# Turning three quarters of a layer's input by VectorE squares and a DRAM exchange instead of one half

## The reference

```
def _layer(x, mem, positions, w_in, ..., w_mem_kv, w_out, ln_g, ln_b):
    (r_q, r_k, r_v, a_cq, a_ckv, a_kpe, l_x, l_v, l_o, l_i, l_f, c_q, z) = _split_cols(x @ w_in, IN_SPLITS)
    ...
    y = jnp.concatenate([ret, mla, mls, memo], axis=-1) * jax.nn.silu(z.astype(f32))
    y = y.astype(x.dtype) @ w_out
    return _layernorm(DEEPNORM_ALPHA * x + y, ln_g, ln_b)
```

## Time and profile before

| | |
|---|---|
| median of 3 runs | 889.2 us (888.85 to 889.35) |
| the profiled execution | 888.95 us, span 887.1 us |
| granted TensorE clock | 1.00 (2.4 GHz) |
| busy: TensorE, VectorE, ScalarE | 881.4, 662.7, 488.6 us |
| HBM traffic | 225 GB/s over the span |

### The profile page before, as it was taken

How to read it: one execution, slowest core, us unless ns; L and a number is a source line. 1 busy time by engine, 2 the same in 40 slices (tenths; PEclk the granted TensorE clock), 3 DMA queues, 4 the chain that set the end, 5 groups by cost and what they waited for, 6 DMA issues and landing times.

```text
span 887.1 us, 13174 instructions
## 1 busy us (share of the span) xinstructions
PE 881.4 (99%) x4516; PEld 757.0 (85%) x4516; DVE 662.7 (75%) x1326; ACT 488.6 (55%) x914; POOL 17.8 (2%) x18
## 2 busy tenths in 40 slices
PE   9999999999999999999999999999999999999997
PEld 8888998888888888888888889888888888888896
DVE  6869697878594677766679787978777878786765
ACT  6655785545455346544477566745355453565641
POOL 0000000000000000000000000000000001000001
PEclk9999999999999999999999999999999999999999
DMA  9796487547669688666677876885485874967822
GB/s 357 289 332 203 136 273 263 170 139 225 214 220 321 214 242 262 201 195 196 191 239 231 295 254 179 263 261 168 140 276 144 280 237 155 291 219 250 329 86 95
DMA packets 72402, 200.33 MB, mean 226 GB/s; under 512 B 9608, under 2 KB 24208, under 8 KB 71696
## 3 DMA queue, kind: packets, MB, share of 16 engines
q1 hardware_dynamic: 71760, 198.44, 68.8%
q10 hardware_dynamic: 576, 1.05, 0.4%
HBM read 183.43 MB, written 16.00 MB: 225 GB/s over the span
## 4 chain that ended last, share of the span: by engine, by line
PE 98%; issue 1%; ACT 0%; POOL 0%; DVE 0%; POOLq 0%; ACTq 0%; DVEq 0%
PE acc L1347 24%; PE acc L1348 24%; PE acc L1351 24%; PE acc L1362 10%; PE acc L1368 5%; PE work L1136 1%; PE work L1135 1%; PE work L1134 1%; PE work L1253 1%; PE work L1252 1%; PE work L1118 0%; PE work L1275 0%; PE work L1264 0%; PE work L1192 0%; PE work L1186 0%
## 5 line engine op out<-in xcount | busy, mean ns | idle before, releaser
L1434 DVE TENSOR_TENSOR lo<-raw,hi 128x512 fp32r<-128x512 f32 (+2 forms) x607 | 387.5, 656 | 181.6 <-ACT hi L1093 174.2
L1093 ACT ACTIVATE hi<-raw 128x512 fp32r<-128x512 f32 (+2 forms) x607 | 356.0, 604 | 297.3 <-PE acc L1351 234.7
L1347 PE MATMUL acc<-hi,xx 128*128 128x512 f32 (+2 forms) x768 | 285.5, 374 | 0.0
L1348 PE MATMUL acc<-hi,xx 128*128 128x512 f32 (+2 forms) x768 | 283.6, 372 | 0.0
L1351 PE MATMUL acc<-lo,xx 128*128 128x512 f32 (+2 forms) x768 | 223.0, 372 | 0.0
L1348 PEld LDWEIGHTS acc<-hi,xx 128*128 128x128 f32 x768 | 144.6, 188 | 23.6
L1347 PEld LDWEIGHTS acc<-hi,xx 128*128 128x128 f32 x768 | 144.6, 188 | 23.6
L1351 PEld LDWEIGHTS acc<-lo,xx 128*128 128x128 f32 x768 | 140.4, 188 | 24.6
L1362 PE MATMUL acc<-xx,hi 128*128 128x512 f32 x384 | 96.0, 392 | 0.0
L1362 PEld LDWEIGHTS acc<-xx,hi 128*128 128x128 f32 x384 | 69.3, 189 | 12.5
L1368 PEld LDWEIGHTS acc<-xx,lo 128*128 128x128 f32 x384 | 52.4, 190 | 3.7
(11 more groups left out here) (348 smaller groups left out, 965.5 us busy)
## 6 DMA issues: line engine op xcount, KB each, us to landing
raw<-in_w SPq DMA_DIRECT2D x263, 512.0 KB, 4.3
B<-turn SPq DMA_DIRECT2D x80, 128.0 KB, 4.2
raw<-in_w SPq DMA_DIRECT2D x26, 256.0 KB, 2.7
turn<-B SPq DMA_DIRECT2D x12, 512.0 KB, 5.6
raw<-in_w SPq DMA_DIRECT2D x16, 328.0 KB, 3.2
turn<-Y SPq DMA_DIRECT2D x8, 512.0 KB, 5.4
Y<-in_wuq SPq DMA_DIRECT2D x2, 1152.0 KB, 9.5
Y<-in_x_t SPq DMA_DIRECT2D x4, 512.0 KB, 8.7
```

The source lines that it names most:

```text
L1093: act.activation(place(l, t, hi), raw[:, s, (t % 2) * w:(t % 2 + 1) * w], ACT.Copy)\
L1347: pe.matmul(o, ah[:, q], hi[:, s, 0:w], start=k == 0, stop=False, skip_group_check=name == "memv")
L1348: pe.matmul(o, al[:, q], hi[:, s, 0:w], start=False, stop=False, skip_group_check=name == "memv")
L1434: dve.tensor_tensor(place(l, t, lo), raw[:, s, (t % 2) * w:(t % 2 + 1) * w], place(l, t, hi).bitcast(F32), ALU.subtract).then_inc(lo_done. ...
```

## The change

The boundary between the two ways moves from column 1024 to column 512. TensorE turns column block 0 alone (`xT` 0 and 1, both at slot 18). VectorE's squares and the DRAM exchange take blocks 1, 2 and 3: `square_x` at slots 10, 12 and 14, writes with pairs 10, 11 and 12, reads with pairs 13, 14 and 15. Each write gets a semaphore of its own, so that the reads of a block wait for its own write. `normalise` goes in the order cb 1, 2, 3, 0. `B` 6 holds the third squares and `B` 7 the turned block 1. `x_hi` and `x_lo` of j = 2 and 3 read it in SBUF and no longer a PSUM bank. The DRAM tensor `x_turn` grows from two blocks to three.

```diff
--- before.py
+++ after.py
@@ -132,7 +132,7 @@
     table.setdefault(slot, []).append(step)
 
 
-for _j in range(4):
+for _j in range(2):
     _put(LATER_PE, 18 + _j // 2 * 4, "xT", _j)
 for _h in range(HEADS):
     _put(PE_AT, (71, 75, 81, 87)[_h], "mem_scores", _h)
@@ -153,7 +153,7 @@
 
 ACT_AT = {}
 for _j in range(8):
-    _put(LATER_ACT, 8 + _j, "normalise", (4, 5, 6, 7, 0, 1, 2, 3)[_j])
+    _put(LATER_ACT, 8 + _j, "normalise", (2, 3, 4, 5, 6, 7, 0, 1)[_j])
     _put(LATER_ACT, (23, 24, 27, 28, 29, 30, 32, 33)[_j], "x_hi", _j)
     _put(FIRST_ACT, 15 + 2 * _j, "x_hi", _j)
     if _j:
@@ -185,8 +185,8 @@
 
 
 DVE_AT = {}
-_put(LATER_DVE, 11, "square_x", 2)
-_put(LATER_DVE, 13, "square_x", 3)
+for _cb in range(1, 4):
+    _put(LATER_DVE, 8 + 2 * _cb, "square_x", _cb)
 for _j in range(8):
     _put(LATER_DVE, (24, 26, 28, 30, 32, 33, 35, 37)[_j], "x_lo", _j)
     _put(FIRST_DVE, 16 + 2 * _j, "x_lo", _j)
@@ -456,11 +456,11 @@
 
         early = [Br[i][:, :].rearrange("p (a k t) -> p a k t", a=2, k=2) for i in (1, 2, 3, 0)]
 
-        x_squares, x_turned = ([B[i][:, 0:1024] for i in pair] for pair in ((4, 5), (2, 0)))
+        x_squares, x_turned = ([B[i][:, 0:1024] for i in pair] for pair in ((4, 5, 6), (7, 2, 0)))
 
         def x_block(j, n):
 
-            return x_turned[j // 2 - 2].rearrange("p (a i j r) -> p j i a r", a=4, i=NT, j=4)[:, j % 2 * 2 + n]
+            return x_turned[j // 2 - 1].rearrange("p (a i j r) -> p j i a r", a=4, i=NT, j=4)[:, j % 2 * 2 + n]
 
         def y_part(part, j):
 
@@ -543,7 +543,7 @@
         first_rows = signal("first_rows", 0)
         finished, gained, diag_done = signal("finished", 0), signal("gained", 0), signal("diag_done", 0)
         scaled, copied = signal("scaled", 0), signal("copied", 0)
-        x_squared, x_turn_out = signal("x_squared", 0), signal("x_turn_out", 0, step=16)
+        x_squared, x_turn_out = signal("x_squared", 0), [signal(f"x_turn_out{cb}", 0, step=16) for cb in (1, 2, 3)]
         stored = signal("stored", 0, step=16)
         dve_own, act_own = signal("dve_own", 0), signal("act_own", 0)
 
@@ -748,14 +748,14 @@
                         wait_job(sp, l, ("ml_q", 1))
                         sp.dma_start(B[3][:, 0:1024], a["mrow"].rearrange("h t -> (h t)").partition_broadcast(P))\
                           .then_inc(mrow_in.sem, 16)
-                    if l and m in (10, 11):
+                    if l and m in (10, 11, 12):
                         sp.wait_ge(x_squared.sem, m - 9)
-                        sp.dma_start(a["x_turn"][m - 10], x_squares[m - 10]).then_inc(x_turn_out.sem, 16)
-                    if l and m in (14, 15):
-                        sp.wait_ge(x_turn_out.sem, 2 * 16)
+                        sp.dma_start(a["x_turn"][m - 10], x_squares[m - 10]).then_inc(x_turn_out[m - 10].sem, 16)
+                    if l and m in (13, 14, 15):
+                        sp.wait_ge(x_turn_out[m - 13].sem, 16)
                         for b in range(4):
-                            sp.dma_start(x_turned[m - 14][b * 32:(b + 1) * 32, :].rearrange("c (a n) -> c a n", a=4),
-                                         a["x_turn"][m - 14, :, b * 256:(b + 1) * 256].rearrange("(a c) n -> c a n", a=4))\
+                            sp.dma_start(x_turned[m - 13][b * 32:(b + 1) * 32, :].rearrange("c (a n) -> c a n", a=4),
+                                         a["x_turn"][m - 13, :, b * 256:(b + 1) * 256].rearrange("(a c) n -> c a n", a=4))\
                               .then_inc(xT_in[m - 12].sem, 16)
                     if m in TURN_OUT_AT:
                         name = TURN_OUT_AT[m]
@@ -862,7 +862,7 @@
                 def normalise(b):
                     cb, i = divmod(b, 2)
                     blk = X[:, i, cb * 512:(cb + 1) * 512]
-                    if b == 4:
+                    if b == 2:
                         act.wait_ge(ln_done.sem, ln_done.at(l, -1))
                     act.activation(blk, blk, ACT.Identity, scale=ln_rstd[:, i:i + 1], bias=ln_shift[:, i:i + 1])\
                        .then_inc(normed.sem, 1)
@@ -879,14 +879,14 @@
                         act.activation(xh[:, 2 * j:2 * j + 2, :], xT0[:, j, :].rearrange("p (k t) -> p k t", k=2),
                                        ACT.Copy).then_inc(x_hi.sem, 1)
                         return
-                    if j < 4:
+                    if j < 2:
                         wait_job(act, l, ("xT", j))
                     else:
                         act.wait_ge(xT_in[j // 2].sem, 16 + 4 * 16)
                     act.wait_ge(cols_in.sem, cols_in.at(l, 0))
                     for k in (2 * j, 2 * j + 1):
-                        o, f = xh[:, k, :], (bank(l, ("xT", j))[:, (k % 2) * 256:(k % 2 + 1) * 256] if j < 4 else x_block(j, k % 2))
-                        m = act.activation(o if j < 4 else o.rearrange("p (i a r) -> p i a r", i=NT, a=4), f, ACT.Identity,
+                        o, f = xh[:, k, :], (bank(l, ("xT", j))[:, (k % 2) * 256:(k % 2 + 1) * 256] if j < 2 else x_block(j, k % 2))
+                        m = act.activation(o if j < 2 else o.rearrange("p (i a r) -> p i a r", i=NT, a=4), f, ACT.Identity,
                                            scale=cols[:, C_LNG + k:C_LNG + k + 1], bias=cols[:, C_LNB + k:C_LNB + k + 1])
                     m.then_inc(x_hi.sem, 1)
 
@@ -1140,7 +1140,7 @@
 
                 def xT(j):
                     pe.wait_ge(ident_in.sem, 16)
-                    pe.wait_ge(normed.sem, 2 * (j // 2) + 6)
+                    pe.wait_ge(normed.sem, 2 * (j // 2) + 8)
                     o = take("xT", j)
                     for kk in range(2):
                         for i in range(NT):
@@ -1484,11 +1484,11 @@
                         dve.wait_ge(cols_in.sem, cols_in.at(l, 0))
                         for k in (2 * j, 2 * j + 1):
                             o, f = tmp[:, (k % 2) * 256:(k % 2 + 1) * 256], \
-                                (bank(l, ("xT", j))[:, (k % 2) * 256:(k % 2 + 1) * 256] if j < 4 else x_block(j, k % 2))
-                            m = dve.tensor_scalar(o if j < 4 else o.rearrange("p (i a r) -> p i a r", i=NT, a=4), f,
+                                (bank(l, ("xT", j))[:, (k % 2) * 256:(k % 2 + 1) * 256] if j < 2 else x_block(j, k % 2))
+                            m = dve.tensor_scalar(o if j < 2 else o.rearrange("p (i a r) -> p i a r", i=NT, a=4), f,
                                                   cols[:, C_LNG + k:C_LNG + k + 1], cols[:, C_LNB + k:C_LNB + k + 1],
                                                   ALU.mult, ALU.add)
-                        if j < 4:
+                        if j < 2:
                             m.then_inc(free_bank(l, "xT", j), 1)
                             wait_read(dve, l, ("xT", j))
                         else:
@@ -1499,8 +1499,8 @@
                         dve.wait_ge(x_lo.sem, x_lo.at(l, j))
 
                 def square_x(cb):
-                    dve.wait_ge(normed.sem, 2 * cb - 2)
-                    to = x_squares[cb - 2].rearrange("p (b i j r) -> p i j b r", b=4, i=NT, j=4)
+                    dve.wait_ge(normed.sem, 2 * cb)
+                    to = x_squares[cb - 1].rearrange("p (b i j r) -> p i j b r", b=4, i=NT, j=4)
                     for i in range(NT):
                         m = dve.transpose(to[:, i], X[:, i, cb * 512:(cb + 1) * 512].rearrange("p (j b c) -> p j b c", j=4, b=4))
                     m.then_inc(x_squared.sem, 1)
@@ -1510,7 +1510,7 @@
                     blk = X[:, i, cb * 512:(cb + 1) * 512]
                     if b == 0:
                         dve.wait_ge(gb0_in.sem, 16)
-                        wait_job(dve, l, ("xT", 3))
+                        wait_job(dve, l, ("xT", 1))
                     link(dve.tensor_tensor(blk, blk, gb0[:, 0, cb * 512:(cb + 1) * 512], ALU.mult))
 
                 def offset(b):
@@ -2076,7 +2076,7 @@
         maps[f"in_{name}"] = v
         args[name] = nc.dram_tensor(f"in_{name}", v.shape, mybir.dt.from_np(v.dtype), kind="ExternalInput").ap()
     args["turn"] = nc.dram_tensor("turn", (len(TURNS), P, 4 * SEQ), F32, kind="Internal").ap()
-    args["x_turn"] = nc.dram_tensor("x_turn", (2, P, 4 * SEQ), F32, kind="Internal").ap()
+    args["x_turn"] = nc.dram_tensor("x_turn", (3, P, 4 * SEQ), F32, kind="Internal").ap()
     args["mrow"] = nc.dram_tensor("mrow", (HEADS, SEQ), F32, kind="Internal").ap()
     out = nc.dram_tensor("out_x", (SEQ, D_MODEL), F32, kind="ExternalOutput").ap()
     build_trunk(nc, args, out)
```

## The result

The changed kernel takes 890.19 us (median of 22 runs, 888.47 to 893.76), the kernel before 889.06 us (22 runs, 888.74 to 890.63). The ratio is 1.0015, 95% interval 1.0009 to 1.0021. I had forecast 888.3 us and minus 0.1%; the sign is wrong and the time lies outside the range. Two things stand beside the median. The fastest execution is 0.27 us faster than the fastest before, so something was gained; and the times now spread over 5.3 us, where they spread over 1.9. The profiled execution took 890.24 us, with a span of 888.4 us. One execution of e5 (2290.86 us) and one of e8 (1483.33 us) lie far outside the rest, and the ranges in the table of experiments leave them out.

The account below looks back on a forecast made before the run. TensorE, busy 881.4 of 887.1 us, was taken as the bound; minus 0.9 us from its transposes and nothing from all other terms took the median from 889.2 to 888.3 us, range 887.8 to 888.8.

Parts of the forecast that it names:

- The removed transposes: TensorE at slot 22: dropping the second group of eight transposes saves 0.9 us, between 0.8 and 1.04 us.
- The rival by which each transpose costs its own 272 ns: TensorE: eight transposes at full length save 2.2 us, giving 887.0 us, faster by 0.25%; chance 0.05.
- VectorE and ScalarE: Squares fit VectorE's gaps at slots 10, 12, 14; ScalarE's +0.18 us falls in a stretch with idle time; both cost nothing.
- SP's queue: Third write and reads issue without a wait, four issues taking 2.0 us; nobody is kept waiting.
- DMA engines: One exchange takes 3.1 us, about 1.25 us pushed behind 468.6; TensorE waits only beyond 3.7 us of slip; cost nothing.
- VectorE's 1.3 us: VectorE's margin after the change between the end of `x_lo` 7 and TensorE's start of slot 38, about 1.3 us.
- It stays to the end because TensorE waits for nobody later: The 0.9 us saved on TensorE in slots 22 to 24 lasts to the kernel's end.
- The slower rival: Late weights: pairs 14 and 15 slip 6.2 us behind the exchange, TensorE waits 2.5 us in slots 30 to 38; 890.8 us; chance 0.05.
- no gain: A wait of about the saved size appears, by slip of about 4.6 us or VectorE's lost margin before slot 38; 889.2 us; chance 0.08.
- ScalarE's idle time ended by a DMA: Sign of being wrong: ScalarE idles at slots 27 to 32 until a DMA ends the wait.
- a later stretch of TensorE off its old pace: Sign of being wrong: a later stretch of TensorE no longer runs at its old pace.
- the 9 us that I had named: Sign of being wrong: landing above 9 us for the loads of pairs 15 and 16.

Follow-up runs that it names:

- e5: The changed kernel with the write of column block 1 but without its four reads; 888.09 us, ratio 0.9989 to the kernel before.
- e8: The kernel before, with layer 1's loads of `wukv` and `wuq` moved one pair later, from 22 to 23; 891.29 us, ratio 1.0024.
- e4: The changed kernel without the write and four reads of column block 1, VectorE's squares kept; 888.25 us, ratio 0.9988 to the kernel before.
- e9: The changed kernel measured again, unaltered; 890.43 us, ratio 1.0010 to the kernel before.
- e1: The changed kernel with layer 1's loads of `wukv` and `wuq` moved from pair 22 to pair 19; 888.60 us, ratio 0.9991 to the kernel before.
- e3: The changed kernel with the eight TensorE transposes put back at slot 22, their result unused; 891.32 us, ratio 1.0016 to the kernel before.
- e6: The changed kernel with column block 1's four reads, from a tensor layer 0 wrote, but without its write; 890.44 us, ratio 1.0012 to the kernel before.
- e2: The kernel before, with layer 1's loads of `wukv` and `wuq` moved from pair 22 to pair 19; 888.92 us, ratio 0.9995.
- e10: The changed kernel with column block 1's four reads, each to 32 partitions, in runs of 4 KB; 890.67 us, ratio 1.0014 to the kernel before.
- e11: The changed kernel with column block 1's four reads replaced by one DMA to 128 partitions, runs of 1 KB; 888.97 us, ratio 0.9990.

## Why the prediction was wrong

- **The removed transposes: right.** 0.89 us from slot 22 to 24 and 0.91 us at slot 38; e4's and e5's fastest runs are 0.8 to 0.9 us below those of before. The rival by which each transpose costs its own 272 ns (2.2 us) fell.
- **VectorE and ScalarE: right by themselves.** The squares do not quite fit the gaps: they delay the `lo` behind them by 0.5 us and with it the loads of pairs 9 to 11 (457.22 for 456.75 at pair 11), and nobody waited for these. The reads of `x_lo` 2 take 0.73 us, `x_hi` 2 takes 1.08 us for its pair. Left alone (e4, e5) they cost nothing.
- **SP's queue: right up to the reads with pair 14.** No wait at pairs 10 to 13. Those reads, however, took 2.94 us to issue, not 2.0, and pair 15 went out 0.6 us late.
- **DMA engines: mis-sized.** I took one exchange for 3.1 us of the engines' time by the mean of two, and it took 5.5 (4.5 in e9). Pair 15 landed 3.0 us later than before, by 0.6 us of later issue and 2.4 us of longer way, where I had 1.25. That mean came from a stretch that ended at 472, with reads still under way. Drawn to 480 it is 6.37 MB less two exchanges, or 8.15 pairs at 1.73 us = 14.1 us, and (21.5 - 14.1) / 2 = 3.7 us for one; the rest of the 5.5 may be what a third costs on top of two, with the engines full. And what is pushed behind 468.6 found no room there: the engines' share in 468.6 to 476 was already 0.98 before. I also followed the wrong load. Pair 15 had 2.4 us to spare, but pair 16, issued at 472.30, landed at 478.5, and `hi` 32 would read it at about 479.5 after the change: 1.0 us to spare. With VectorE's 1.3 us the limit for pair 16 was about 2.3 us of slip, not 3.7. It slipped by 2.6 us. In the profiled execution TensorE just missed waiting at slot 38, with VectorE's margin down to 0.16 us, and in other kernels' executions (e1, e3, e6) it was gone.
- **"It stays to the end because TensorE waits for nobody later": the step that failed.** No wait in the profile before means only that each margin is at least zero. One of them, 0.69 us at slot 46, was smaller than the gain, and it hangs on a load that is issued behind VectorE's `lo`. Making TensorE 0.9 us earlier and VectorE 0.3 us later needed 1.2 us there even if the load had landed as fast as before; it took 1.0 us longer. e8 (1.0024) shows the deadline by itself, and e2 (spread gone) goes with it.
- **The rivals.** The slower rival had the right mechanism (late weights behind the exchange) with the wrong place and size: I put it at slots 30 to 38 and 1.6 us, it came out at 46, and 1.1 us. I gave it 0.05, and "no gain" by a lost margin 0.08. Of the signs that I named for being wrong, two came: ScalarE's idle time ended by a DMA at slots 30 and 32, and a later stretch of TensorE off its old pace. Landing stayed at 8.7 and 8.8 us, under the 9 us that I had named.

What stays open: why four DMAs to 32 partitions cost more than a wide one. e10 and e11 differ in the tensor that they read and in the number of issues too. The tensor is unlikely: e6 reads in four narrow DMAs from the same tensor `turn` as e11 and has the loss. The number of issues is not tested.

## What to carry to other kernels

Before counting a gain on the engine that bounds the kernel, walk on from it and write down the margin of every load that the bound engine's feeders wait for; a feeder that already waits for a DMA in the profile (here 1.47 us, with 0.69 us left behind it) caps the gain. An exchange through DRAM should be priced by the stretch in which it is the only extra traffic, writes and reads apart, and its queue's neighbours carry the price. Where a time gets more scattered after a change, look for a deadline that is now met by chance.

## What the hardware showed that I had not expected

- The same 512 KB cost the DMA engines 2.1 us as one write from 128 partitions and 4.0 us as four reads to 32 partitions each; the wide read made the loss go away, longer runs did not. The Trainium skill (SBUF — State Buffer, section Door 1: The DMA port swizzle) says that a DMA to 32 partitions reaches 8 of the 16 ports and gives 189 GB/s against 328 for 128 partitions, both for transfers of 1 MiB. e10 and e11 agree with its direction, by ratios of 1.0014 and 0.9990 and by pair 15's 9.0 and 7.8 us to landing; no run here measures one DMA alone.
- In the stretch with a share of 1.03 issuing slowed as well: one read of the turned input held SP's queue for 1.51 us, where the longest of these reads before took 0.58 us. That the full engines are the reason is not tested.
- Full engines moved only 233 GB/s in 468.6 to 476 of the changed kernel, and 412 GB/s with a share of 1.02 in the loads at 5 to 25 us.
